# Mixer stage in another step order: two score products ahead of the last q projection, the next unit's scores between transposes and value products

## What is computed

```python
x = x + 0.5 * swiglu(rms(x, g_ffn1), w_up1, w_down1)
h = rms(x, g_mix);  z = h @ w_in          # q | k | v | f | gate_a | gate_b
y_a = window_attention(q, k, v, sink, rel_bias) @ w_branch_a
y_b = real(fft2(f over positions and group channels)) @ w_branch_b
x = x + (sigmoid(gate_a) * y_a + sigmoid(gate_b) * y_b) @ w_out
x = x + 0.5 * swiglu(rms(x, g_ffn2), w_up2, w_down2)
return rms(x, g_final)
```

## Time and profile before

| | |
|---|---|
| median of three runs | 1013.02 us (1012.06 to 1014.2) |
| profiled execution, time | 1014.11 us |
| profiled execution, span | 1012.3 us |
| TensorE busy | 997.7 us, 99% of the span |
| VectorE, ScalarE, GpSimd busy | 679.0, 440.1, 198.1 us |
| mean granted TensorE clock | 0.995 of full speed |

### The profile page before, as it was taken

How to read it: one execution, slowest core, us unless ns; L and a number is a source line. 1 busy time by engine, 2 the same in 40 slices (tenths; PEclk the granted TensorE clock), 3 DMA queues, 4 the chain that set the end, 5 groups by cost and what they waited for, 6 DMA issues and landing times. The chain is left out here.

```text
span 1012.3 us, 16276 instructions
## 1 busy us (share of the span) xinstructions
PE 997.7 (99%) x5872; PEld 885.7 (87%) x5872; DVE 679.0 (67%) x924; ACT 440.1 (43%) x656; POOL 198.1 (20%) x113
## 2 busy tenths in 40 slices
PE   8999999999999999999999999999999999999997
PEld 7789999999788888888888888888999999978887
DVE  5778999999534346667765555458899999943332
ACT  5344444446322325346664334334445454633322
POOL 2452333340011110000000001324234333001101
PEclk9999999999999999999999999999999999999999
DMA  6423334323433364212213343322333332333222
GB/s 210 132 66 94 116 92 120 87 83 96 124 96 90 115 171 125 63 42 62 63 42 89 98 124 104 104 84 72 96 108 100 110 97 83 89 117 96 88 68 84
DMA packets 191816, 98.81 MB, mean 98 GB/s; under 512 B 13384, under 2 KB 190616, under 8 KB 191648
## 3 DMA queue, kind: packets, MB, share of 16 engines
q1 hardware_dynamic: 190560, 95.50, 32.3%
q10 hardware_dynamic: 1216, 2.78, 0.8%
HBM read 96.15 MB, written 2.11 MB: 97 GB/s over the span
## 5 line engine op out<-in xcount | busy, mean ns | idle before, releaser
L575 ACT ACTIVATE w_hi<-raw 128x1024 fp32r<-128x1024 f32 (+2 forms) x202 | 181.5, 902 | 231.6 <-PE bank L1496 155.2
L953 DVE TENSOR_TENSOR w_lo<-raw,w_hi 128x1024 fp32r<-128x1024 f32 (+2 forms) x138 | 150.0, 1089 | 145.7 <-ACT w_hi L575 144.2
L1595 PE MATMUL bank<-t_lo,w_hi 128*128 128x256 f32 x896 | 224.7, 283 | 0.0
L1593 PE MATMUL bank<-t_hi,w_hi 128*128 128x256 f32 x896 | 224.6, 283 | 0.0
L1595 PEld LDWEIGHTS bank<-t_lo,w_hi 128*128 128x128 f32 x896 | 172.0, 192 | 0.2
L1593 PEld LDWEIGHTS bank<-t_hi,w_hi 128*128 128x128 f32 x896 | 172.0, 192 | 0.2
L1430 POOL TENSOR_TENSOR ssum<-ssum,sq 128x512 f32<-128x512 f32 x27 | 41.4, 1533 | 535.2 <-ACT sq L612 534.4
L1599 PE MATMUL bank<-t_hi,w_lo 128*128 128x256 f32 x896 | 144.0, 283 | 0.0
L1484 PE MATMUL bank<-a_hi,w_hi 128*128 128x512 f32 (+1 forms) x374 | 140.6, 380 | 1.7 <-ACT a_hi L575 1.7
L1485 PE MATMUL bank<-a_lo,w_hi 128*128 128x512 f32 (+1 forms) x374 | 139.4, 377 | 0.0
L1599 PEld LDWEIGHTS bank<-t_hi,w_lo 128*128 128x128 f32 x896 | 123.6, 192 | 0.0
(11 more groups left out here) (230 smaller groups left out, 1494.6 us busy)
## 6 DMA issues: line engine op xcount, KB each, us to landing
raw<-in_w_down_dram SPq DMA_DIRECT2D x48, 384.0 KB, 3.0
raw_b<-in_w_up_dram SPq DMA_DIRECT2D x64, 256.0 KB, 3.7
raw<-in_w_up_dram SPq DMA_DIRECT2D x64, 256.0 KB, 3.6
raw<-in_w_up_dram SPq DMA_DIRECT2D x24, 512.0 KB, 3.9
raw<-in_w_in_dram SPq DMA_DIRECT2D x22, 512.0 KB, 3.7
raw<-in_w_down_dram SPq DMA_DIRECT2D x32, 128.0 KB, 2.2
raw<-in_w_out_dram SPq DMA_DIRECT2D x8, 512.0 KB, 3.4
x_rows<-in_x_dram SPq DMA_DIRECT2D x4, 512.0 KB, 7.8
```

Of the source, the lines that this page charges most:

```text
L575: return nc.scalar.activation(dst, src, ACT.Copy, scale=scale)
L953: vec.tensor_tensor(w_lo[:, s, 0:nk, :], raw[:, s, 0:nk, :], w_hi[:, s, 0:nk, :].bitcast(F32), ALU.subtract).then_inc(w_lo_ready, 1)
L1593: nc.tensor.matmul(out_ap, w_hi[:, slot, at_ + k, :], hi[:, k, :], start=first and k == 0, stop=False, skip_group_check=not first)
L1595: nc.tensor.matmul(out_ap, w_hi[:, slot, at_ + k, :], lo_[:, k, :], start=False, stop=False, skip_group_check=not first)
```

## The change

The diff moves steps in the `MIXER` list and changes two things that the new order asks for. In the list: `scores 0 0` and `scores 0 1` go ahead of `q 3`; `scores 0 2` and `0 3` go behind the first quarter of the first gate; in units 1 to 6 single gate quarters, branch halves and value products change places, and in units 2, 3, 4 and 6 the last two scores of a unit go between a transpose (or a value product) and the value product that followed it. Beside it, `B_B` starts with bank 0 instead of 1, so that the first gate granule waits for the reading of q 2 and not of q 3, and the third granule of each pair in the loop behind the list (bank 0) waits for one more bank read. No instruction is added or taken away.

```diff
--- before.py
+++ after.py
@@ -78,7 +78,7 @@
 B_CH, B_POS = 4, 6
 B_S = 4
 B_PT, B_O = [2, 6], 3
-B_B = [1, 0, 7]
+B_B = [0, 1, 7]
 
 HALF = SEQ // 2
 
@@ -161,24 +161,23 @@
 
 MIXER = """
     f 0; f 1; f 2; f 3; channels 0; k; v; positions 0; channels 1; q 0; positions 1; channels 2; q 1;
-    positions 2; channels 3; q 2; turn_v; positions 3; q 3;
-    scores 0 0; scores 0 1; gate_b 0 0 0; gate_b 0 0 1; scores 0 2; scores 0 3; max 0; gate_b 0 0 2; exp 0;
+    positions 2; channels 3; q 2; turn_v; positions 3; scores 0 0; scores 0 1; q 3;
+    gate_b 0 0 0; scores 0 2; scores 0 3; max 0; gate_b 0 0 1; gate_b 0 0 2; exp 0;
     scores 1 0; normalize 0; gate_b 0 0 3; gate_b 0 1 0; scores 1 1; turn 0 0; turn 0 1; scores 1 2;
-    gate_b 0 1 1; values 0 0; scores 1 3; max 1; values 0 1; exp 1; normalize 1; gate_b 0 1 2; gate_b 0 1 3;
-    branch_b 0 0 0; sigmoid 0;
-    scores 2 0; scores 2 1; turn 1 0; branch_b 0 0 1; turn 1 1; branch_b 0 1 0; values 1 0; values 1 1;
-    scores 2 2; scores 2 3; max 2; take_b 0 0; exp 2; normalize 2; branch_b 0 1 1; gate_b 1 0 0; gate_b 1 0 1;
+    gate_b 0 1 1; values 0 0; scores 1 3; max 1; gate_b 0 1 2; values 0 1; exp 1; normalize 1; gate_b 0 1 3; branch_b 0 0 0; sigmoid 0;
+    scores 2 0; scores 2 1; turn 1 0; branch_b 0 0 1; turn 1 1; branch_b 0 1 0; values 1 0; scores 2 2; scores 2 3;
+    values 1 1; max 2; take_b 0 0; exp 2; normalize 2; branch_b 0 1 1; gate_b 1 0 0; gate_b 1 0 1;
     take_b 0 1; gate_b 1 0 2; gate_b 1 0 3; turn 2 0; turn 2 1;
-    scores 3 0; scores 3 1; gate_b 1 1 0; values 2 0; turn 2 2; values 2 1; scores 3 2; scores 3 3; max 3;
-    exp 3; normalize 3; gate_b 1 1 1; gate_b 1 1 2; gate_b 1 1 3; values 2 2; sigmoid 1;
+    scores 3 0; scores 3 1; gate_b 1 1 0; values 2 0; turn 2 2; scores 3 2; scores 3 3; values 2 1; max 3;
+    exp 3; normalize 3; gate_b 1 1 1; gate_b 1 1 2; values 2 2; gate_b 1 1 3; sigmoid 1;
     scores 4 0; branch_b 1 0 0; turn 3 0; turn 3 1; scores 4 1; branch_b 1 0 1; values 3 0; turn 3 2;
-    values 3 1; scores 4 2; scores 4 3; max 4; exp 4; take_b 1 0; branch_b 1 1 0; normalize 4; values 3 2;
+    scores 4 2; scores 4 3; values 3 1; max 4; exp 4; take_b 1 0; branch_b 1 1 0; normalize 4; values 3 2;
     branch_b 1 1 1; gate_b 2 0 0;
-    scores 5 0; scores 5 1; take_b 1 1; gate_b 2 0 1; turn 4 0; turn 4 1; gate_b 2 0 2; gate_b 2 0 3;
-    values 4 0; values 4 1; turn 4 2; scores 5 2; scores 5 3; max 5; exp 5; normalize 5; gate_b 2 1 0;
+    scores 5 0; scores 5 1; take_b 1 1; gate_b 2 0 1; turn 4 0; turn 4 1; gate_b 2 0 2; values 4 0; gate_b 2 0 3;
+    turn 4 2; values 4 1; scores 5 2; scores 5 3; max 5; exp 5; normalize 5; gate_b 2 1 0;
     values 4 2; gate_b 2 1 1; gate_b 2 1 2; gate_b 2 1 3; branch_b 2 0 0; turn 5 0; turn 5 1;
-    scores 6 0; scores 6 1; values 5 0; turn 5 2; values 5 1; scores 6 2; scores 6 3; max 6; exp 6;
-    branch_b 2 0 1; values 5 2; normalize 6; branch_b 2 1 0; branch_b 2 1 1; sigmoid 2; take_b 2 0; take_b 2 1;
+    scores 6 0; scores 6 1; branch_b 2 0 1; values 5 0; turn 5 2; scores 6 2; scores 6 3; values 5 1; max 6; exp 6;
+    branch_b 2 1 0; values 5 2; normalize 6; branch_b 2 1 1; sigmoid 2; take_b 2 0; take_b 2 1;
     gate_b 3 0 0; gate_b 3 0 1; turn 6 0;
     scores 7 0; turn 6 1; gate_b 3 0 2; scores 7 1; values 6 0; scores 7 2; scores 7 3; values 6 1; max 7;
     exp 7; normalize 7; gate_b 3 0 3; gate_b 3 1 0; gate_b 3 1 1; gate_b 3 1 2; gate_b 3 1 3; turn 7 0;
@@ -1781,7 +1780,7 @@
                         pair, i, quarter = step[1:]
                         n = SLOTS * pair + i
                         if quarter == 0:
-                            pe.wait_ge(out_read, O_B + n - 2 if n else O_B)
+                            pe.wait_ge(out_read, O_B + n - 2 if n > 1 else O_B - 1 + n)
                         granule(G_B + n, banks[B_B[n % 3]][:, :], h_parts, first=quarter == 0, last=quarter == 3,
                                 tiles=range(2 * quarter, 2 * quarter + 2), done=quarter == 3)
                     elif kind == "branch_b":
@@ -1803,7 +1802,7 @@
                         if j == 1:
                             pe.wait_ge(o_lo_ready, TB * N_KV)
                         o = O_A + j
-                        pe.wait_ge(out_read, o - 3 + SLOTS * pair)
+                        pe.wait_ge(out_read, o - (2 if j == 2 else 3) + SLOTS * pair)
                         granule(G_A + j, banks[o % BANKS][:, :],
                                 (lambda k: (qo_hi[:, k, :], qo_lo[:, k, :])) if j % 2 else h_parts,
                                 it=pair, n=SLOTS)
```

## The result

The changed kernel takes 1016.62 us (median of 8 runs, 1015.87 to 1020.5), the kernel before 1012.66 us in the same comparison (8 runs): the ratio is 1.0046, with a 95% interval of 1.0034 to 1.0059. The forecast was 1017.0 us, slower by 4.0. The profiled execution of the changed kernel took 1018.0 us with a span of 1016.2 us.

The account below looks back on a forecast made before the run. TensorE, busy 99% of the span, was taken as the bound. Terms summed to 3.8 us, taken as 4.0 with small read waits, on 1013.02: 1017.0 us; own range 1016.2 to 1018.0, 8 in 10 from 1014.4 to 1019.2.

Parts of the forecast that it names:

- turn 0 0 later: Unit 0: new TensorE waits for v's low part (1.11 us) and the last q's (2.06) put turn 0 0 1.72 us later.
- turn 1 0 on top: Unit 1: values 0 1 behind a gate quarter delays ScalarE's copy and exponentials; turn 1 0 waits, +1.1 us.
- scores 3 2 and 3 3, to turn 3 0: Moved scores 3 2 and 3 3 wait for VectorE's reads of score banks: +0.55 us.
- values 3 0, to turn 4 0: values 3 0 waits for its low part, delayed by the earlier values 2 2: +0.25 us, between 0 and +0.5.
- values 4 0 and turn 5 0: values 4 0 a quarter earlier meets its low part, +0.1 us, and delays unit 5's probabilities, +0.4; bounds 0 and 0.8.
- values 5 0 and turn 6 0: The wait of values 5 0 goes behind branch_b 2 0 1, -0.8 us; later probabilities hold turn 6 0, +0.5.
- to turn 7 0: From turn 6 0 to turn 7 0: no term, as unit 7 isn't changed.
- read waits of scores 4 3, 6 2, 6 3: Small bank read waits at these scores, 0.05 to 0.1 us each, taking the sum from 3.8 to 4.0 us.
- one fall of the clock, as a rival: TensorE's clock falls after the gap before scores 0 3: 1.65 us more, 1018.7 us; chance 0.15.
- only the two early terms hold: Rival: turn 0 0 and turn 1 0 terms hold, later units break even: 1015.8 us; chance 0.14.
- v comes earlier: No-change rival: short wait for v before the first scores, only scores 0 3 costs, 0.6 us: 1013.6 us; chance 0.12.
- the splits keep pace: Faster rival: v's and the last q's low parts come early, early waits and values 5 0's are won: 1010.7 us; chance 0.07.

Follow-up runs that it names:

- changed again: The changed kernel as it is, run once more on one chip with the gap-filled kernel: 1.0053 of the kernel before, median 1017.49 us; its trace had no clock fall.
- e3: Against the changed kernel, values 0 1 ahead of gate_b 0 1 2 again: 1.0037 of the kernel before, median 1016.23 us.
- e1: Against the changed kernel, scores 0 0 and 0 1 behind q 3 again and first gate quarters as before: 1.0027 of the kernel before, median 1014.92 us.
- e7: Against the kernel before, only branch_b 2 0 1 moved ahead of values 5 0: ratio 0.9997.
- e5: Against the changed kernel, scores 0 2 and 0 3 behind three gate quarters instead of one: 1.0039 of the kernel before.
- e8: Against the kernel before, only q 3 moved ahead of positions 3: ratio 0.9986, median 1011.09 us against 1012.99.
- e6: Against the kernel before, scores 0 2 and 0 3 ahead of gate_b 0 0 1, q 3 and banks as they were: ratio 1.0005.

## Why the prediction was right, point by point

| step | forecast, us | measured | from |
|---|---|---|---|
| turn 0 0 later | +1.72 | +1.87 | changed again |
| turn 1 0 on top | +1.1 | +1.04, and none in e3 | changed again, e3 |
| scores 3 2 and 3 3, to turn 3 0 | +0.55 | +0.56 | changed again |
| values 3 0, to turn 4 0 | +0.25 | +0.24 | changed again |
| values 4 0 and turn 5 0 | +0.5 | +0.71 | changed again |
| values 5 0 and turn 6 0 | -0.3 | -0.31 | changed again |
| to turn 7 0 | 0 | +0.18 | changed again |
| read waits of scores 4 3, 6 2, 6 3 | +0.2 | within the rows above | |
| sum | 4.0 | 4.27 | |
| one fall of the clock, as a rival | 1.65 | 1.60 | the two traces of the changed kernel |

**The start.** The wait for v came at its place, 1.00 and 1.04 us of idle time for 1.11, and so did that for the last q, 1.92 and 1.91 for 2.06 (the list's idle time is shorter than what is lost: from 441.10 to 443.29 a matmul of 0.12 us takes 2.19, so 2.07 are lost). turn 0 0 came 0.15 us later than forecast. Of this 0.09 stood at the wait for v: I had let a release show on TensorE 0.05 us later. In the repeated trace that holds for the last q, but v's low part is written at 434.51 and TensorE starts at 434.65, 0.14 later (0.15 in the first trace):

```profile
433.82 0.69 DVE L956 TENSOR_TENSOR v_lo<-bank,v_hi 128x512 fp32r<-128x512 f32 x1
443.60 0.69 DVE L956 TENSOR_TENSOR qo_lo<-ga_t,qo_lo 64x512 fp32r<-64x512 f32 x1
```

Why the two differ, no run shows. The other 0.06 us aren't traced to one place.

**Unit 1.** The mechanism is shown by e3: taking one quarter back out of the way of one copy on ScalarE takes the whole wait away.

**Units 2 to 6.** The rows were right within 0.25 us, the places in part. The bank wait stood at scores 3 2, as forecast: the four transposes ahead of it take 0.36 us, and it starts 0.73 us after the first of them, when VectorE is through with the read of scores 3 0.

```profile
477.39 0.60 PE L1760 MATMUL bank<-ident,s_a 128*128 128x128 f32 x4
478.12 0.45 PE L1747 MATMUL bank<-kp_hi,qo_lo 128*128 128x384 f32 x1
```

values 3 0 was held before its first matmul (0.18 us more than in the kernel before) and not at its third. I had turn 5 0 wait 0.4 us for its probabilities and gave values 4 0 0.1. The turn lost only 0.16 us; values 4 0, a quarter earlier and so onto its low part, lost 0.30; and 0.25 went at values 4 2, which the forecast didn't name. Its low part VectorE wrote behind the delayed split of the gate's weights that the forecast does name. In the repeated trace:

```profile
501.34 0.39 PE L1775 MATMUL bank<-pt_hi,v_lo 128*128 128x512 f32 x1
501.76 0.50 PE L1777 MATMUL bank<-pt_lo,v_hi 128*128 128x512 f32 x1
...
506.94 0.40 PE L1775 MATMUL bank<-pt_hi,v_lo 128*128 128x512 f32 x1
507.32 0.50 PE L1777 MATMUL bank<-pt_lo,v_hi 128*128 128x512 f32 x1
```

The first two are of values 4 0: 0.42 us lie between two starts that are 0.23 apart undisturbed, and 0.11 more go behind it. values 4 2 repeats it with 0.15 and 0.10. No line of the list of waits holds these; only distances between starts show them. No run undoes the moves of units 2 to 5 one by one: their sizes rest on the traces, their sum on e1.

**Unit 7.** I had said that it isn't changed. Its steps aren't, but e7 loses 0.16 us between turn 6 0 and turn 7 0 in the same way: after the moved branch VectorE reads scores 7 1 0.19 us later against turn 6 0, and scores 7 3, which needs that bank, loses 0.18 us where it lost 0.03. This is the term that was missing.

**The clock.** I kept the fall out of the forecast and gave it 0.15. The size was right (1.60 for 1.65), but the question was put wrongly: it is not a property of the kernel but of the execution. The two traces of the changed kernel hold one answer each. The median, 3.96 us over the kernel before with an interval of 3.4 to 6.0, fits the waits alone, 4.27; the repeat was 4.5 us over (4.1 to 6.6). That the first median met the forecast within 0.04 us is luck, since waits and clock differ from the forecast by more than that.

**The rivals.** That only the two early terms hold fell: e1, without the front, is left with 2.40 us at the loop, 1.08 of unit 1 and 1.3 of the later units. That v comes earlier fell with the 1.0 us wait. That the splits keep pace, the faster side, fell at the last q. One sum of the prediction is off, without weight for the forecast: the four waits it lists cost 0.58, 0.58, 0.36 and 0.82 us, which makes 2.3 us to be won at most in that stretch, not some 3.

## What to carry to other kernels

When an engine is busy 99% of the time, as here, a new order gains or loses at its waits (and at what the clock does behind them), and most can be worked out before the order is tried: write down when the data are ready on the other engines, and when the moved step arrives. Look for the chain and not for the wait: filling the largest gap (e5) won 0.4 of 1.9 us, since the next step of the same chain waited in its place, while starting the chain earlier (e8) won 0.8 us. In a list that several engines share, a step moved for one engine also moves a copy on another, and what stands behind that copy may be the next unit's critical work.

## What the runs showed of the hardware

TensorE's clock can fall to 1.2 GHz for a stretch like that from 443.30 to 446.70 us behind a single wait of 1.9 us in an otherwise full stream, in some executions (three of four traces) and not in others of the same kernel; each fall cost 1.6 us. Waits of 1.62 us (e6) and of 1.13 us (e5) had no fall behind them, in one trace each, nor did the same gap when it was filled with eight unneeded matmuls (two traces). A wait costs TensorE 0.07 to 0.11 us beyond its length, at the distance to the next matmul: the first score product after the wait for v starts at 433.61 and the next at 433.80, 0.19 us later, where 0.12 is usual; in the kernel before a 512-column matmul starts after its wait at 440.81 and the next at 441.15, 0.34 us later, where 0.23 is usual.
